# Splitting the last output panel and the next head into token halves in a two-layer transformer trunk

## Chip, cores and metric

One core of one Trainium2 chip runs the whole program. The metric is the device time of one execution in microseconds (us), median of three runs; lower is better.

## The reference, cut to what matters

The trunk has 272 tokens (16 meta tokens in front of 256), width 1024 and two layers of three sub-layers each: SwiGLU, mixer, SwiGLU. The mixer of layer 0 is stick-breaking attention, that of layer 1 sliding-window attention. Everything is float32. Each sub-layer has a norm before and a norm after:

```python
def rms_norm(x, g):
    y = x * lax.rsqrt(jnp.mean(x * x, axis=-1, keepdims=True) + RMS_EPS)
    return y * g

def swiglu(x, w_gate, w_up, w_down):
    return (jax.nn.silu(x @ w_gate) * (x @ w_up)) @ w_down

f = swiglu(rms_norm(h, g[0]), ...)
h = h + 0.5 * rms_norm(f, g[1])
m = mixer(rms_norm(h, g[2]), ...)
h = h + rms_norm(m, g[3])
f = swiglu(rms_norm(h, g[4]), ...)
h = h + 0.5 * rms_norm(f, g[5])
```

So at each of the five boundaries between sub-layers the output f of one is squared and summed over the width for each token, scaled by the inverse root, added to the residual h, and the sum is normed again for the first products of the next sub-layer. The second norm's factor depends on the token alone, so it is applied after the products.

## The kernel before, in words

Activations lie transposed: the width on the partitions, in 8 blocks of 128 (index d or k), the tokens along the free axis (272 columns; 256 where the meta tokens are no longer needed, in the output of sub-layer 4 and in sub-layer 5). Sub-layers are numbered u = 0 to 5: ffn, sb (stick-breaking), ffn, ffn, swa (sliding window), ffn.

Weights come in 156 panels of 1 MB (128 partitions by 2048). SyncE loads a panel into one of two `raw` slots (L484) as soon as the panel two before is wholly converted. ScalarE rounds it to fp32r (`w_hi`, L553, two halves of 1024 columns), and VectorE takes the rest (`w_lo`, L821, two halves). There are four converted slots, so ScalarE may start on panel g when TensorE has finished panel g - 4 (semaphore `panel_done`). Each product is made of three matmuls with fp32r operands (`three`, L1219 to L1224): w_lo with y_hi, w_hi with y_hi, w_hi with y_lo. Each of them has a weight load of its own.

An ffn sub-layer has 22 input panels (each gives 2 blocks of 128 rows, from 8 blocks k) and 11 output panels. An output panel covers 2 blocks of the hidden width and adds to all 8 output blocks d: 8 x 2 x 3 = 48 matmuls of 272 columns (`out_panel`, L1631). sb and swa have 4 output panels each with the same 48 matmuls (`out_column`, L1415; `out_unit`, L1542, 256 columns).

The boundary goes like this. During the last output panel, each block d that is done signals `f_done`. ScalarE squares the blocks (L784, L792, L797) and copies some to SBUF (L779). VectorE adds the squares (L1148 to L1164) and copies the others (L1168). After its last product TensorE sums over the partitions by multiplying with ones, in two token halves (`post_sums`, L1659 to L1665, plain float32, three calls for a half), and then runs two matmuls whose result nobody reads (L1669, `IDLE`). ScalarE turns each half's sum into the factor by Ln and Exp (L804, L807). VectorE makes y_hi of block 0 by a short way (L1176, L1180), then its y_lo (L1184, L1186), then for the other blocks the scaled output (L1197) and the new residual (L1204). ScalarE makes y_hi of it (L567) and VectorE y_lo (L833).

TensorE meanwhile waits for y_hi of block 0 and then runs the head of the next sub-layer: its first three panels at once, k by k, so that block k is needed as late as possible. For each k there are 6 tiles (3 panels x 2), with 12 matmuls on y_hi (L1287, L1289) and 6 on y_lo (L1296), all over the full 272 or 256 columns. At k = 7 a matmul with ones (L1275) sums the squares for the second norm. The fourth panel and the rest follow.

The order of each engine is written out by hand, with semaphores; instructions run in the order of the text. In an ffn sub-layer ScalarE and VectorE convert, in the loop ahead of the boundary, all three panels of the next head (`n_split`, L461); after sb and swa the third panel is converted during the boundary.

Of the kernel before, what the change touches and what calls it, by code (L numbers as in the profile page):

```python
# [25 lines left out]
P = 128  # L26
D = 1024
KT = D // P
SEQ = 256
META = 16  # L30
L = META + SEQ
# [72 lines left out]
SW_LO = [2] + [1] * 9 + [2, 2, 2]  # L104
SW_OUT = [(6, 0), (6, 1), (7, 0), (7, 1), (5, 0), (5, 1), (0, 0), (1, 0)]
SW_FILL = {6: [(0, 0), (0, 1)], 7: [(0, 2)], 8: [(1, 0), (1, 1)], 9: [(1, 2)], 10: [(0, 3), (1, 3), (2, 0)], 11: [(2, 1)]}
SW_LAST = [(2, 2), (2, 3)]
# [46 lines left out]
def bank_out(t):  # L154

    return [0, 1, 2, 3, 4, 5, 6, 7] if t.kind == "sb" else [4, 5, 6, 7, 0, 1, 2, 3]

def out_tile(ps, t, d):  # L160

    if t.kind == "swa":
        bank, half = SW_OUT[d]
        return ps[:, bank, 256 * half:256 * half + 256]
    return ps[:, bank_out(t)[d], t.t_out:L]


def out_pair(ps, t, n):

    if t.kind == "swa" and n < 3:  # L170
# [3 lines left out]
    b0 = bank_out(t)[2 * n]  # L174
    return ps[:, b0:b0 + 2, t.t_out:L]


def stays(t, d):

    return t.kind == "swa" and d < 4  # L180
# [8 lines left out]
X_ORDER = [1, 0, 2, 3, 4, 5, 6, 7]  # L189


def bank_half(t):

    return (2, 3) if t.kind == "swa" else (bank_out(t)[2], bank_out(t)[1])


def bank_idle(t):

    return 4 if t.kind == "swa" else bank_out(t)[3]
# [8 lines left out]

IDLE = 2
# [9 lines left out]
def build(nc, first_in, x_in, gains_in, sinks_in, row_in, panels_in, const_in, out):  # L219
    ctx = ExitStack()  # L220
    with ctx:
# [143 lines left out]
        f_saved2 = sem("f_saved2")  # L365
# [9 lines left out]
        part_ready = sem("part_ready")  # L375
# [85 lines left out]
        def n_split(t):  # L461

            return min(t.n_out - 1, PANELS - t.g_out - SLOTS)
# [80 lines left out]
        def _(a):  # L544
# [16 lines left out]
            def split_y(b):  # L561

                t0 = SUBS[b].t_in

                for d in range(KT if b == 0 else 1, KT):
                    a.wait_ge(x_ready, KT * (b - 1) + X_ORDER.index(d) + 1)
                    nc.scalar.activation(y_hi[:, d, t0:L], xT[:, d, t0:L], ACT.Copy,  # L567
                                         scale=gains[:, SUBS[b].pre + d:SUBS[b].pre + d + 1]).then_inc(yh_ready, 1)
                if b == 0:
                    conv_hi(2)  # L570
                    a.wait_ge(x_landed, 16)
                for c in range(2):
                    nc.scalar.activation(fT[:, 4 * c:4 * c + 4, t0:L], xT[:, 4 * c:4 * c + 4, t0:L],
                                         ACT.Square).then_inc(x_sq, 1)
# [30 lines left out]
            split_y(0)  # L605

            for t in SUBS:
# [141 lines left out]
                if t.kind == "ffn":  # L749
                    steps(a, n_split(t), lambda i, it: conv_hi(t.g_out + i + 4, it))  # L750
                elif t.kind == "sb":
                    conv_hi(t.end)
                    conv_hi(t.end + 1)
                    hi_half(t.end + 2, 0)
# [21 lines left out]
                k = t.u  # L776
                t0 = t.t_out
                def save_f(n):
                    nc.scalar.copy(fT[:, 2 * n:2 * n + 2, t0:L], out_pair(ps, t, n))\  # L779
                        .then_inc(f_saved, 3 if stays(t, 0) else 1)  # L780

                for n in range(2):
                    a.wait_ge(f_done, KT * k + 2 * n + 2)
                    nc.scalar.activation(sq[:, 2 * n:2 * n + 2, t0:L], out_pair(ps, t, n), ACT.Square)\  # L784
                        .then_inc(f_sq, 1)
                    if t.kind == "swa" and n == 0:
                        hi_half(t.end + 2, 0)
                    if not stays(t, 2 * n):
                        save_f(n)
                for d in range(4, 7):  # L790
                    a.wait_ge(f_done, KT * k + (6 if t.kind == "swa" and d == 4 else d + 1))
                    nc.scalar.activation(sq[:, d, t0:L], out_tile(ps, t, d), ACT.Square).then_inc(f_sq, 1)  # L792
                    if d == 5 and t.kind == "ffn":
                        save_f(2)
                a.wait_ge(f_done, KT * k + KT)
                for c0, c1 in token_halves(t):
                    nc.scalar.activation(sq[:, 7, c0:c1], out_tile(ps, t, 7)[:, c0 - t0:c1 - t0],  # L797
                                         ACT.Square).then_inc(f_sq, 1)
                if t.kind != "ffn":
                    save_f(2)  # L800

                for i, (c0, c1) in enumerate(token_halves(t)):
                    a.wait_ge(post_sum, 2 * k + i + 1)
                    nc.scalar.activation(post_ln[:, c0:c1], ps[:, bank_half(t)[i], c0:c1], ACT.Ln,  # L804
                                         scale=t.factor ** -2 / D).then_inc(post_log, 1)
                    a.wait_ge(post_log, 2 * k + i + 1)
                    nc.scalar.activation(post_f[:, c0:c1], post_ln[:, c0:c1], ACT.Exp, scale=-0.5).then_inc(post_ready, 1)  # L807
                if t.kind != "ffn":
                    hi_half(t.end + 2, 1)
                if t.u < 5:  # L810
                    split_y(t.u + 1)
# [3 lines left out]
        def _(v):  # L815
# [14 lines left out]
            def y_low(b, d):  # L830
                t0 = SUBS[b].t_in
                v.wait_ge(yh_ready, KT * b + d + 1)
                nc.vector.scalar_tensor_tensor(  # L833
                    out=y_lo[:, d, t0:L], in0=xT[:, d, t0:L],
                    scalar=gains[:, SUBS[b].pre + d:SUBS[b].pre + d + 1],
                    in1=y_hi[:, d, t0:L].bitcast(F32), op0=ALU.mult, op1=ALU.subtract).then_inc(yl_ready, 1)

            def pre_norm(b):
# [3 lines left out]
                v.wait_ge(x_sq, 2 * b + 2)  # L842
                for n, m in enumerate((4, 2, 1)):
                    nc.vector.tensor_tensor(fT[:, 0:m, t0:L], fT[:, 0:m, t0:L], fT[:, m:2 * m, t0:L],
                                            ALU.add).then_inc(x_acc, 1)
                    v.wait_ge(x_acc, 3 * b + n + 1)
# [32 lines left out]
            conv_lo(2)  # L879
            pre_norm(0)  # L880
# [3 lines left out]
            for t in SUBS:  # L884
# [217 lines left out]
                elif t.kind == "sb":  # L1102
                    conv_lo(t.end)
                    conv_lo(t.end + 1)
                    lo_half(t.end + 2, 0)
                if t.u == 5:
# [12 lines left out]
                    def result(n):  # L1119
# [25 lines left out]
                k, t0 = t.u, t.t_out  # L1145

                v.wait_ge(f_sq, 7 * k + 2)
                nc.vector.tensor_tensor(sq[:, 0:2, t0:L], sq[:, 0:2, t0:L], sq[:, 2:4, t0:L],  # L1148
                                        ALU.add).then_inc(f_acc, 1)
                v.wait_ge(f_acc, 4 * k + 1)  # L1150

                if t.kind == "ffn":
                    nc.vector.scalar_tensor_tensor(out=sq[:, 0, t0:L], in0=eps_ms[:, t0:L], scalar=float(KT),
                                                   in1=sq[:, 0, t0:L], op0=ALU.mult, op1=ALU.add).then_inc(f_acc, 1)
                else:
                    nc.vector.tensor_scalar(sq[:, 0, t0:L], sq[:, 0, t0:L], KT * EPS, None,
                                            ALU.add).then_inc(f_acc, 1)
                v.wait_ge(f_acc, 4 * k + 2)

                v.wait_ge(f_sq, 7 * k + 4)  # L1160
                nc.vector.tensor_tensor(sq[:, 0:2, t0:L], sq[:, 0:2, t0:L], sq[:, 4:6, t0:L],
# [625 lines left out]
```

## Time and profile before

| what | value |
|---|---|
| time, median of 3 runs | 1038.69 us (1038.0 to 1039.81) |
| profiled execution, span from first to last instruction | 1036.6 us (no other time of it is shown) |
| TensorE (PE) busy | 1024.9 us, 99% of the span, 8028 matmuls |
| weight loads (PEld) busy | 994.0 us, 96%, 8028 loads |
| VectorE (DVE) busy | 641.2 us, 62% |
| ScalarE (ACT) busy | 517.6 us, 50% |
| GpSimd (POOL) busy | 16.7 us, 2% |
| DMA | 171.26 MB, mean 165 GB/s |
| five boundaries, start of the first ones-matmul | 206.4, 342.1, 545.4, 748.7, 838.7 us |

How to read it: the profile is of one execution. Times are us from the start of its span unless ns is written. Matmuls are pipelined: the recorded length of one (0.29 us) is longer than the distance from its start to the start of the next, and it is that distance which counts when many follow each other. A matmul in plain float32 appears as two instructions, one with fp32r operands as one. The median of the runs lies 2.1 us above the profiled span.

### The profile page before, as it was taken

Reading aid. Unit: us, or ns where it says so; the run is one execution under the profiler, and the core shown is the slowest. Engines: PE = TensorE matmul, PEld = TensorE weight load, DVE = VectorE, ACT = ScalarE, POOL = GpSimd, SP = SyncE. Lnnn points to the kernel's source line nnn. Section 1 sums busy time; section 2 is a strip of 40 time slices with the busy share of each in tenths; the row PEclk is TensorE's granted clock in tenths of the full one; section 3 lists DMA queues with packets and bytes.
Section 4 is the critical chain, followed back from the end, with each engine's and each line's share of the span. In section 5 each row is a group of like instructions: output and inputs, shape, how many; then the busy total and the mean of one; then the engine's idle time right before and its main releaser. Section 6 shows DMA issues by size and latency. Waiting matters only on the chain.

```text
span 1036.6 us, 19946 instructions
## 1 busy us (share of the span) xinstructions
PE 1024.9 (99%) x8028; PEld 994.0 (96%) x8028; DVE 641.2 (62%) x893; ACT 517.6 (50%) x740; POOL 16.7 (2%) x28
## 2 busy tenths in 40 slices
PE   9999999999999999999999999999999999999997
PEld 8999999999999999999999999999998899999886
DVE  6765553478775876554447755543589777765533
ACT  5643443446675564434345544443447755544433
POOL 0000000000000000000000000000023000000000
PEclk9999999999999999999999999999999999999999
DMA  8665555514333266445542755445513335655451
GB/s 328 218 228 167 187 174 166 183 58 148 138 127 118 82 208 236 164 164 186 178 163 82 239 174 191 166 167 183 179 41 123 121 125 194 233 181 198 168 183 41
DMA packets 24533, 171.26 MB, mean 165 GB/s; under 512 B 2976, under 2 KB 2976, under 8 KB 4384
## 3 DMA queue, kind: packets, MB, share of 16 engines
q1 hardware_dynamic: 24048, 169.49, 47.4%
q8 instruction: 41, 0.67, 0.3%
q10 hardware_dynamic: 432, 1.00, 0.2%
q14 instruction: 12, 0.10, 0.0%
HBM read 169.43 MB, written 1.05 MB: 164 GB/s over the span
## 4 chain that ended last, share of the span: by engine, by line
PE 95%; DVE 2%; ACT 2%; DMA 0%; issue 0%; DVEq 0%; POOL 0%; SPq 0%; ACTq 0%; POOLq 0%
PE ps L1222 25%; PE ps L1224 25%; PE ps L1223 25%; PE ps L1287 2%; PE ps L1296 2%; PE ps L1289 2%; PE ps L1594 2%; PE ps L1595 2%; PE ps L1593 2%; PE ps L1353 1%; PE ps L1408 1%; PE ps L1527 1%; PE ps L1499 1%; PE ps L1235 1%; DMA raw<-in_panels_dram 0%; PE ps L1515 0%
## 5 line engine op out<-in xcount | busy, mean ns | idle before, releaser
L553 ACT CAST w_hi<-raw 128x1024 fp32r<-128x1024 f32 x312 | 312.7, 1047 | 393.7 <-PE ps L1224 299.4
L821 DVE TENSOR_TENSOR w_lo<-raw,w_hi 128x1024 fp32r<-128x1024 f32 x312 | 370.2, 1225 | 191.0 <-ACT w_hi L553 190.5
L1222 PE MATMUL ps<-y_hi,w_lo 128*128 128x272 f32 (+1 forms) x1454 | 420.8, 289 | 0.1
L1224 PE MATMUL ps<-y_lo,w_hi 128*128 128x272 f32 (+1 forms) x1454 | 417.8, 287 | 0.0
L1223 PE MATMUL ps<-y_hi,w_hi 128*128 128x272 f32 (+1 forms) x1454 | 416.2, 286 | 0.0
L1222 PEld LDWEIGHTS ps<-y_hi,w_lo 128*128 128x128 f32 x1454 | 273.9, 188 | 1.9 <-issue 1.1
L1223 PEld LDWEIGHTS ps<-y_hi,w_hi 128*128 128x128 f32 x1454 | 273.9, 188 | 0.3
L1224 PEld LDWEIGHTS ps<-y_lo,w_hi 128*128 128x128 f32 x1454 | 274.0, 188 | 0.0
L1222 PE MATMUL ps<-h_hi,w_lo 128*128 (+1 forms) x528 | 152.1, 288 | 0.0
L1223 PE MATMUL ps<-h_hi,w_hi 128*128 (+1 forms) x528 | 152.0, 288 | 0.0
L1224 PE MATMUL ps<-h_lo,w_hi 128*128 (+1 forms) x528 | 151.3, 286 | 0.0
L1223 PEld LDWEIGHTS ps<-h_hi,w_hi 128*128 128x128 f32 x528 | 99.4, 188 | 0.0
L1222 PEld LDWEIGHTS ps<-h_hi,w_lo 128*128 128x128 f32 x528 | 99.4, 188 | 0.0
L1224 PEld LDWEIGHTS ps<-h_lo,w_hi 128*128 128x128 f32 x528 | 99.4, 188 | 0.0
L899 DVE TENSOR_TENSOR hid<-act,ps 128x544 f32<-128x544 f32 (+1 forms) x44 | 31.2, 710 | 70.3 <-PE ps L1224 70.3
L894 DVE TENSOR_TENSOR act<-ps,rms_inv 128x544 f32<-128x544 f32 (+1 forms) x44 | 31.5, 716 | 55.7 <-PE ps L1224 50.3
L1287 PE MATMUL ps<-y_hi,w_lo 128*128 128x272 f32 (+1 forms) x210 | 54.3, 291 | 3.4 <-DVE y_hi L1180 2.8
L1289 PE MATMUL ps<-y_hi,w_hi 128*128 128x272 f32 (+1 forms) x210 | 53.2, 286 | 0.0
L1287 PEld LDWEIGHTS ps<-y_hi,w_lo 128*128 128x128 f32 x210 | 39.5, 188 | 6.5 <-DVE y_hi L1180 4.9
L1289 PEld LDWEIGHTS ps<-y_hi,w_hi 128*128 128x128 f32 x210 | 39.5, 188 | 0.0
L567 ACT ACTIVATE y_hi<-xT,gains 128x272 fp32r<-128x272 f32 (+1 forms) x35 | 18.2, 521 | 35.1 <-DVE xT L1204 35.1
L1594 PE MATMUL ps<-w_hi,h_hi 128*128 128x512 f32 x88 | 34.7, 395 | 0.0
(192 smaller groups left out, 1051.4 us busy)
## 6 DMA issues: line engine op xcount, KB each, us to landing
raw<-in_panels_dram SPq DMA_DIRECT2D x156, 1024.0 KB, 4.9
first<-in_first_dram SPq DMA_DIRECT2D x3, 784.0 KB, 6.8
xT<-in_x_dram SPq DMA_DIRECT2D x1, 1088.0 KB, 13.4
out_dram<-fT SPq DMA_DIRECT2D x4, 256.0 KB, 2.0
const<-in_const_dram ACTq DMA_DIRECT2D x1, 920.0 KB, 10.2
first<-in_first_dram SPq DMA_DIRECT2D x2, 392.0 KB, 3.6
gain_row<-in_row_dram SPq DMA_DIRECT2D x1, 512.0 KB, 5.5
gains<-in_gains_dram ACTq DMA_DIRECT2D x1, 48.0 KB, 3.6
```

The lines of the kernel that those rows point to most:

```text
L553: nc.scalar.copy(w_hi[:, g % SLOTS, part], raw_part(g, part)).then_inc(hi_ready, 1)
L821: nc.vector.tensor_tensor(w_lo[:, g % SLOTS, part], raw_part(g, part), w_hi[:, g % SLOTS, part].bitcast(F32), ALU.subtract).then_inc(lo_re ...
L894: nc.vector.tensor_tensor(act[:, j % 2, :, t0:L], ps[:, b0:b0 + 2, t0:L], spread(rms_inv, 2, t0), ALU.mult).then_inc(gate_ready, 1)
L899: nc.vector.tensor_tensor(hid[:, j % 2, :, t0:L], act[:, j % 2, :, t0:L], ps[:, b0:b0 + 2, t0:L], ALU.mult).then_inc(h_ready, 1)
L1222: nc.tensor.matmul(dst, w_lo[:, slot, pc], yh, start=first, stop=False, skip_group_check=shared)
L1223: nc.tensor.matmul(dst, w_hi[:, slot, pc], yh, start=False, stop=False, skip_group_check=shared)
L1224: return nc.tensor.matmul(dst, w_hi[:, slot, pc], yl, start=False, stop=last, skip_group_check=shared)
L1287: nc.tensor.matmul(dst, w_lo[:, g % SLOTS, pc], y_hi[:, k, c0:L], start=(k == 0), stop=False)
L1289: nc.tensor.matmul(dst, w_hi[:, g % SLOTS, pc], y_hi[:, k, c0:L], start=False, stop=False)
L1296: nc.tensor.matmul(ps[:, BANK_IN[i][c], c0:L], w_hi[:, g % SLOTS, pc], y_lo[:, k, c0:L], start=False, stop=False)
L1593: nc.tensor.matmul(dst, hh[:, cols], w_lo[:, slot, at:at + 512], start=first, stop=False)
L1594: nc.tensor.matmul(dst, hh[:, cols], w_hi[:, slot, at:at + 512], start=False, stop=False)
```

## The change

The last output panel runs over the left token half for all 8 blocks d and then over the right half (136 columns each, 128 in swa), instead of once over all columns. The three ones-calls of the left half come after the third or fourth block of the right half, those of the right half after the first k of the next head's left half. The head's first two k (`SPLIT = 2`) run in halves too: left on y_hi, left on y_lo, right on y_hi, right on y_lo; k = 2 to 7 stay whole. At the boundary after swa one of the six tiles, (2, 0), runs its first two k whole and late. ScalarE and VectorE square, add, save and scale in halves where the halves are apart. The second half of the third head panel is converted later, after the fourth step over the blocks, and after an ffn sub-layer its first half too comes at the start of the boundary. The squares for the second norm are made in four pairs instead of two fours. The idle matmuls are gone. Banks in PSUM are dealt out anew: blocks 6 and 7 (4 to 7 in swa) are read by VectorE from PSUM instead of from a copy. The core of the diff:

```diff
-            return min(t.n_out - 1, PANELS - t.g_out - SLOTS)
+            return min(t.n_out - 2, PANELS - t.g_out - SLOTS)
...
+                def last_panel():
+
+                    k, g = t.u, t.end - 1
+                    pe.wait_ge(lo_ready, 2 * g + 2)
+                    for half, (c0, c1) in enumerate(token_halves(t)):
+                        for d in range(KT):
+                            if half == 1:
+                                if stays(t, d) or t.kind == "swa" and d >= 4:
+                                    pe.wait_ge(f_sq, 10 * k + (3 if d < 6 else 5 if t.kind == "swa" else d - 2))
+                                elif d // 2 == 1:
+                                    pe.wait_ge(f_saved_d, 2 * k + 1)
+                                else:
+                                    pe.wait_ge(f_saved, 4 * k + (1 if d < 2 else 2))
+                                if t.kind != "swa" and d == KT - 1:
+                                    pe.wait_ge(post_log, 2 * k + 1)
+                            for c in range(2):
...
+                                mm = three(out_tile(ps, t, d)[:, c0 - t0:c1 - t0], g % SLOTS, D * c + P * d, hh, hl,
+                                           False, c == 1, shared=True)
                             mm.then_inc(f_done, 1)
...
-                    if t.u < 5:
-                        for _ in range(IDLE):
-                            nc.tensor.matmul(ps[:, bank_idle(t), t0:L], cst("ones"), sq[:, 0, t0:L], start=True, stop=True)
+                            if half == 1 and d == SUM_AFTER[t.kind]:
+                                post_sums(t, 0)
...
+                    for k in range(SPLIT):
+                        pe.wait_ge(yha_ready, Y_LEFT * n + k + 1)
+                        for tile in early:
...
+                            mm = head_part(tile, k, left, 0, first=(k == 0))
+                            if k == 0 and tile == (0, 0):
+                                mm.then_inc(panel_done, 1)
+                            head_part(tile, k, left, 1)
+                        if k == 0:
+                            post_sums(prev, 1)
+                    for k in range(SPLIT):
+                        pe.wait_ge(yla_ready, SPLIT * n + k + 1)
+                        for tile in early:
+                            head_part(tile, k, left, 2)
+                    for k in range(SPLIT):
+                        pe.wait_ge(yh_ready, KT * t.u + k + 1)
+                        for tile in early:
+                            head_part(tile, k, right, 0)
+                            head_part(tile, k, right, 1)
+                    for k in range(SPLIT):
                         pe.wait_ge(yl_ready, KT * t.u + k + 1)
...
+                        for tile in early:
+                            head_part(tile, k, right, 2)
+                    for tile in late:
+                        pe.wait_ge(post_log, 2 * n + 2)
+                        for k in range(SPLIT):
+                            for part in range(3):
+                                head_part(tile, k, (t0, L), part, first=(k == part == 0))
+                    for k in range(SPLIT, KT):
...
```

ScalarE's new order at the boundary:

```diff
+                hi_half(t.end + 2, 0)
+                square_pair(0, 0)
+                square_pair(1, 0)
+                save_pair(0, 0)
+                square_pair(2, 0)
...
+                    square_tile(6, 0)
+                    square_tile(7, 0)
+                    save_pair(2, 0)
+                square_pair(0, 1)
+                square_pair(1, 1)
+                factor(0)
+                save_pair(1, 1)
+                square_pair(2, 1)
...
+                    save_pair(2, 1)
+                    square_tile(6, 1)
+                    square_tile(7, 1)
+                y_high(k + 1, 0)
+                factor(1)
+                y_high(k + 1, 1)
```

and VectorE's:

```diff
+                lo_half(t.end + 2, 0)
+                add_squares(0)
+                add_last(0)
+                save_pair(1, 0)
+                fold(0)
+                save_pair(0, 1)
+                add_squares(1)
...
+                first_high(0)
                 u_of(0)
...
+                x_of(0)
+                add_last(1)
+                fold(1)
+                first_low(0)
+                y_low(b, 1, 0)
+                v.wait_ge(f_saved_d, 2 * k + 1)
+                u_of(1)
+                x_of(1)
+                first_high(1)
+                u_of(2)
+                x_of(2)
+                first_low(1)
```

## Rows read from the trace of the kernel before

**Rows 1.** The page, part 1 and the granted clock over 40 slices.

```profile
PE 1024.9 (99%) x8028; PEld 994.0 (96%) x8028; DVE 641.2 (62%) x893; ACT 517.6 (50%) x740; POOL 16.7 (2%) x28
...
PEclk9999999999999999999999999999999999999999
```

**Rows 2.** The page, chain that ended last, shares by engine.

```profile
PE 95%; DVE 2%; ACT 2%; DMA 0%; issue 0%; DVEq 0%; POOL 0%; SPq 0%; ACTq 0%; POOLq 0%
```

**Rows 3.** Waits of TensorE: total us, times, longest.

```profile
PE ps L1287 <- DVE y_hi L1180: 2.8, 5, 0.6
```

**Rows 4.** Timeline, first boundary: start, length, engine, line.

```profile
202.82 0.29 PE L1224 MATMUL ps<-h_lo,w_hi 128*128 128x272 f32 x1
...
206.18 0.28 PE L1224 MATMUL ps<-h_lo,w_hi 128*128 128x272 f32 x1
...
207.22 0.31 PEld L1659 LDWEIGHTS ps<-sq,const 128*128 128x128 f32 x2
...
207.91 0.76 PEld L1669 LDWEIGHTS ps<-sq,const 128*128 128x128 f32 x4
...
209.66 0.39 PE L1287 MATMUL ps<-y_hi,w_lo 128*128 128x272 f32 x1 [0.55 <-DVE y_hi L1180]
...
210.01 0.28 PE L1287 MATMUL ps<-y_hi,w_lo 128*128 128x272 f32 x1
...
211.26 0.92 PE L1296 MATMUL ps<-y_lo,w_hi 128*128 128x272 f32 x6
...
212.63 0.29 PE L1287 MATMUL ps<-y_hi,w_lo 128*128 128x272 f32 x1
```

**Rows 5.** Timeline, fifth boundary (after swa).

```profile
838.54 0.28 PE L1224 MATMUL ps<-sw_lo,w_hi 128*128 128x256 f32 x1
...
842.80 0.28 PE L1287 MATMUL ps<-y_hi,w_lo 128*128 128x256 f32 x1
...
843.98 0.87 PE L1296 MATMUL ps<-y_lo,w_hi 128*128 128x256 f32 x6
...
845.32 0.28 PE L1287 MATMUL ps<-y_hi,w_lo 128*128 128x256 f32 x1
```

**Rows 6.** Timeline, running sums of sb: fp32r matmuls of 64 columns among wider ones.

```profile
241.85 0.19 PE L1393 MATMUL ps<-sp_hi,sums_w 128*128 128x64 f32 x1
241.85 0.19 PEld L1395 LDWEIGHTS ps<-sp_hi,sums_w 128*128 128x128 f32 x1
241.88 0.27 PE L1395 MATMUL ps<-sp_hi,sums_w 128*128 128x64 f32 x1
241.96 0.19 PEld L1385 LDWEIGHTS ps<-sp_lo,sums_w 128*128 128x128 f32 x1
241.99 0.36 PE L1385 MATMUL ps<-sp_lo,sums_w 128*128 128x256 f32 x1
242.07 0.19 PEld L1387 LDWEIGHTS ps<-sp_lo,sums_w 128*128 128x128 f32 x1
242.19 0.28 PE L1387 MATMUL ps<-sp_lo,sums_w 128*128 128x256 f32 x1
```

**Rows 7.** Groups of ACT and DVE by line: busy us, mean ns, idle before.

```profile
L553 ACT CAST w_hi<-raw 128x1024 fp32r<-128x1024 f32 x312 | 312.7, 1047 | 393.7 <-PE ps L1224 299.4
L821 DVE TENSOR_TENSOR w_lo<-raw,w_hi 128x1024 fp32r<-128x1024 f32 x312 | 370.2, 1225 | 191.0 <-ACT w_hi L553 190.5
...
L792 ACT ACTIVATE sq<-ps 128x272 f32<-128x272 f32 (+1 forms) x15 | 5.9, 405 | 1.3 <-PE ps L1224 1.1
...
L807 ACT ACTIVATE post_f<-post_ln 128x136 f32<-128x136 f32 (+1 forms) x10 | 3.1, 315 | 0.3
...
L1180 DVE TENSOR_TENSOR y_hi<-sq,pre_ms 128x136 fp32r<-128x136 f32 (+1 forms) x10 | 3.0, 298 | 0.3
L1176 DVE SCALAR_TENSOR_TENSOR sq<-fT,gg,post_f 128x136 f32<-128x136 f32 x8 | 2.8, 356 | 3.5 <-ACT post_f L807 3.5
```

**Rows 8.** DMA issues: size and median us from issue to landing.

```profile
raw<-in_panels_dram SPq DMA_DIRECT2D x156, 1024.0 KB, 4.9
```

More of the change, by code:

```diff
@@ L173, in out_pair @@
         return ps[:, 0:2, 0:256]
-    b0 = bank_out(t)[2 * n]
-    return ps[:, b0:b0 + 2, t.t_out:L]
+    return ps[:, 2 * n:2 * n + 2, t.t_out:L]
 def stays(t, d):
-    return t.kind == "swa" and d < 4
+    return d >= (4 if t.kind == "swa" else 6)
 def token_halves(t):
@@ L775, in _ @@
                     break
[L776 to L798, printed above, removed]
@@ new lines, in _ @@
+                if t.kind == "swa":
+                    square_pair(3, 1)
+                else:
+                    save_pair(2, 1)
[4 more added lines that the diff above has]
+                y_high(k + 1, 1)
+                for i in range(2, X_OPS):
+                    if X_ORDER[i][0] > 0:
+                        y_high(k + 1, i)
+                    if i == 3:
+                        hi_half(t.end + 2, 1)
+                    for n, after in SQUARES:
+                        if after == X_ORDER[i][0] and i >= 4:
+                            if n == 0:
+                                a.wait_ge(x_ready, X_OPS * k + 8)
+                            x_square(n, t0)
@@ L814, in _ @@
+                norm_x(k + 1)
         @block.vector
@@ new lines, in _ @@
+                v.wait_ge(f_saved, 4 * k + (2 if t.kind == "swa" else 4))
+                u_of(3)
+                x_of(3)
+                y_low(b, 1, 1)
+                u_of(4)
+                y_low(b, 2)
+                x_of(4)
+                u_of(5)
+                x_of(5)
+                y_low(b, 3)
+                lo_half(t.end + 2, 1)
+                for i in range(6, X_OPS):
+                    u_of(i)
+                    x_of(i)
+                    if i != 8:
+                        y_low(b, {6: 4, 7: 5, 9: 6}[i])
+                    else:
+                        add_pair(b, 0)
@@ new lines, in head_part @@
+                def head_part(tile, k, cols, part, first=False, last=False):
+                    i, c = tile
+                    g, (c0, c1) = t.g0 + i, (max(cols[0], first_col(t, i)), cols[1])
+                    if part == 0:
+                        pe.wait_ge(lo_ready, 2 * g + 1 + k // 4)
+                    pc = slice(256 * k + P * c, 256 * k + P * c + P)
+                    return nc.tensor.matmul(ps[:, BANK_IN[i][c], c0:c1], (w_lo if part == 0 else w_hi)[:, g % SLOTS, pc],
+                                            (y_lo if part == 2 else y_hi)[:, k, c0:c1], start=first, stop=last,
+                                            skip_group_check=True)
```

409 lines of the change are left out of this document (222 added, 187 removed).

## The prediction

> **What bounds the kernel now.** I read the page first. TensorE is busy for 99% of the span at the full granted clock (9 in all 40 slices, 2.4 GHz) [rows 1], and the chain that ended last lies on it for 95% [rows 2]. So a microsecond of TensorE work costs a microsecond, and only its pauses can be won. The list of its waits gives 2.8 us in five waits for y_hi of block 0, one for each boundary [rows 3]. That list understates them, since the ones-matmuls and the idle ones fill most of the pause. So I took the pause from the timeline [rows 4]: 202.82 to 206.18 holds 27 products, which gives 0.1244 us from start to start. The last product of sub-layer 0 starts at 206.18 and the third of the next head at 210.01. Less three distances that is 3.46 us without products. A second, small pause stands before k = 1: the six y_lo matmuls start at 211.26, so the ninth start after that should be at 212.26 (eight distances) and is at 212.63, 0.38 us late. The next three boundaries show 3.46 to 3.47 and 0.35 to 0.43. The one after swa has 256 columns and a distance of 0.118 us (ten in 842.80 to 843.98); its pause is 842.80 - 838.54 - 3 x 0.118 = 3.91 us, and 845.32 - 843.98 - 8 x 0.118 = 0.40 follow [rows 5]. Together 4 x 3.46 + 3.91 + 4 x 0.38 + 0.40 = 19.7 us.
>
> **What is removed.** The ones-calls stay: three for a half take 207.22 to 207.91 = 0.69 us [rows 4], six 1.38, and at five boundaries 6.9 us. If products cover all the rest, 19.7 - 6.9 = 12.8 us go. That is the whole prize. The idle matmuls are inside it: four instructions issued from 207.91, over before y_hi arrives at 209.66, so they cost nothing, and taking them out gives nothing of its own. The clock was full on both sides of the pause, and in the new order no pause of that length is left in which it could fall.
>
> **What is added: matmuls.** The last panel is 48 matmuls at full width, and becomes 96 at half width. The head's first two k are 2 x 6 x 3 = 36 and become 72 (at the fifth boundary one tile stays whole: 30 become 60). Over five boundaries 5 x 48 + 4 x 36 + 30 = 414 whole ones go and 828 halves come. The columns are the same; the number of weight loads doubles, since each matmul has its own load (8028 and 8028) [rows 1]. Of the whole ones 324 have 272 columns (four panels of 48, three heads of 36, 24 of the head of swa) and 90 have 256 (the other 12 of that head, 78 at the fifth boundary): 324 x 0.1244 + 90 x 0.118 = 50.9 us.
>
> What does a half cost? The trace has no 136-column fp32r matmul. The nearest rows are two of 64 columns in the running sums [rows 6]. The first starts at 241.85, and the next is let in at 241.88: 64 columns stream in 0.03 us, so narrow fp32r is not slower for each column. But its weights are being loaded from 241.85, the next load begins at 241.96 and the one after at 242.07: 0.11 us from load to load, though the matmuls between them need 0.03. The loads set the pace. Seen in four such places the two steps take 0.22 or 0.23, so **0.1125 us for each half**, against 0.1244 for a whole. A half streams in 136/64 x 0.027 = 0.057 us, well under the load, and cannot go below it. Bounds: 0.107 (the shortest step that the two-digit rows allow) to 0.118 (the distance at 256 columns [rows 5]). The far end below is the half's own streaming plus what a whole one has over its columns: 272 columns at the rate of rows 6 are 0.113, so 0.011 on top, 0.068 in all. The far end above is a ones-call of 136 columns, 0.69 / 3 = 0.23 us [rows 4]. I take 0.1125, because rows 6 are the same type, the same 128x128 weights and the only place where a matmul is shorter than its load.
>
> 828 x 0.1125 = 93.2 us, less 50.9: **+42.3 us**, of which 24.5 in the panels and 17.8 in the heads. Net 42.3 - 12.8 = **+29.5 us**.
>
> The Trainium skill speaks to this in "TensorE: Matmul & The Clock Gate". Its section "LDWEIGHTS (loading the stationary operand)" has a load take its columns divided by 1.2 GHz, 107 ns for 128; rows 6 agree (0.11 us). Its section "Back-to-back issue gap" is milder: about 81 ns for each load and matmul pair at 128 columns. By that figure the sum would be 828 x 0.081 - 50.9 - 12.8 = +3.4 us instead of +29.5; rows 6 speak against it, and no other row bears on it.
>
> **Do the other engines keep up?** Count from the start of the last panel, at 0.1125. The left half ends at 5.4 us, three blocks of the right take 2.0, the sums 0.7, the other five 3.4: the head's first product is due at 11.5. ScalarE converts half a panel first (1.05 [rows 7]), then squares pairs as they come (0.41 for 272 elements). With the left's last square at 5.9, a copy, the right's first pair to 7.4 and its second, released by block 3 of the right half at 8.8, to 9.4, Ln (about 0.3) and Exp (0.32) end at 10.0. VectorE needs 0.36 + 0.30 [rows 7] and a passing of semaphores, so y_hi of block 0, left, is there at about 11.0, 0.5 before it is due. The right sums need the last square (12.0) at 12.8 and the added squares (12.4) at 13.3. y_hi of block 1, left, comes at 12.3 and is due at 13.5; the right half of block 0 at 15.2, due at 16.2; that of block 1 at 16.2, due at 17.6. From k = 2 a step is 18 x 0.1244 = 2.24 us for TensorE and some 1.4 for VectorE, as before. The moved conversion costs ScalarE 1.05 and VectorE 1.23 us once [rows 7] near k = 3, and its result is first needed at k = 4, 3 us later. The load that this releases, panel end + 4, takes 4.9 us [rows 8] and its slot is read more than 10 us later. SyncE and GpSimd issue nothing else. So the terms are priced at nothing under that cover, with margins of 0.5 to 1 us; if the ScalarE line slips (the queue behind the wait for the left sums holds the right half's squares), each boundary waits 0.5 to 1.5 us more. The four pairs of squares instead of two fours add two instructions off the path.
>
> **The sum.** Profiled span 1036.6 + 29.5 = 1066.1 us. The median of the runs is 2.1 above that span, so 1038.7 + 29.5 = **1068.2 us**. With 0.107 and 0.118 for a half it is 1063.6 and 1072.8.
>
> **Rivals.**
> 1. Weights are loaded ahead and a half costs its own streaming, 0.068 us. Then 828 x 0.068 = 56.3, +5.4 - 12.8 = -7.4: **1031 us**, faster. It decides below (50.9 + 12.8) / 828 = 0.077 us for a half. For it: the recorded length of a load, 0.19 us, is longer than the distance, so loads do overlap matmuls. Against it: rows 6, where two short matmuls in a row did not bring the loads closer than 0.11. And at that pace the pair of ScalarE and VectorE would be late at block 0 and give part of it back, up to no change. Chance 0.06 faster, 0.03 within 0.2%.
> 2. Loads overlap in part, and a half costs between 0.077 and 0.107 us: at the middle, 0.092, it is 76.2 - 50.9 - 12.8 = +12.5, **1051 us**. For it: rows 6 are only two matmuls long, and a long row of short ones may settle at a closer pace. Chance 0.06. The 81 ns of the Trainium skill's section "Back-to-back issue gap" would lie at its lower end.
> 3. The forecast's load pace, and the margins of the paragraph above are not there: a wait of 0.5 to 1.5 us at each boundary on y_hi of block 0 or on the right half's sums, **1071 to 1076 us**. For it: five engine hand-overs in the chain. Chance 0.15.
> 4. Narrow fp32r is as slow as the ones-calls: 828 x 0.23 - 50.9 - 12.8 = +127, **1165 us**. Rows 6 speak against it (64 columns in 0.03 us). Chance 0.04.
>
> **How the numbers follow.** The forecast has 0.66. Two runs of this kernel can be told apart above 0.2% (2.1 us). Faster by more: 0.06. Within: 0.03. Slower: 0.66 + 0.15 + 0.06 + 0.04 = 0.91. The range takes in the forecast's bounds, nearly all of rival 3, and some room below for a load pace slightly under 0.107: 1055 to 1078 holds about 0.8.
>
> **What would show it.** In the changed kernel's profile: PE and PEld instructions both up by 414 less the 20 idle ones; 96 matmuls of 136 columns over about 10.8 us in each last panel (6.0 before), 0.11 apart; loads of 128x128 back to back without gaps there; no wait for y_hi of block 0 at a boundary; from the start of the last panel to the end of k = 7 some 34 us (28 before). If the half-width matmuls stand less than 0.077 apart, the forecast is wrong in sign; if TensorE shows idle stretches at the boundary, the margins are wrong; if the whole-width matmuls change their distance, the cause lies elsewhere.

## The result, and the profile after

The changed kernel takes **1068.76 us** (median of 4 runs, 1067.69 to 1069.14) against 1038.76 for the kernel before in the same session (4 runs). The ratio is 1.0287, with an interval of 1.0273 to 1.0302: slower, by 30.0 us, where 29.5 were forecast. The profiled execution has a span of 1067.3 us and took 1069.12.

The page of the changed kernel, its span, the busy times and the granted clock [rows 1], and the shares of the chain that ended last [rows 2]:

```profile
span 1067.3 us, 20900 instructions
...
PE 1056.7 (99%) x8422; PEld 1030.6 (97%) x8422; DVE 650.9 (61%) x954; ACT 522.2 (49%) x780; POOL 16.8 (2%) x28
...
PEclk9999999999999999999999999999999999999999
...
PE 97%; ACT 1%; DVE 1%; DMA 1%; issue 0%; DVEq 0%; SPq 0%; ACTq 0%
```

PE and PEld both went up by 394, which is the forecast 414 less the 20 idle ones. TensorE was the bound before and is it still, at the full clock. A share of 99% before and after says nothing of whether the work in it got dearer; the distances do. TensorE's waits in the changed kernel [rows 3]:

```profile
PE ps L1356 <- ACT y_hi L605: 1.5, 1, 1.5
PE ps L1340 <- POOL post_ln L503: 1.1, 1, 1.1
PE ps L1327 <- DVE qkv L961: 0.9, 1, 0.9
PE ps L1543 <- DVE sp_lo L994: 0.6, 1, 0.6
PE ps L1657 <- DVE qkv L1086: 0.6, 1, 0.6
```

The five waits for y_hi at the boundaries are gone. L1356 lies in the first sub-layer, which the change does not touch. L961 (first tile of sb behind its head) and L1086 (the scores of swa) are new; where they come from stands in the part on why the prediction was right. The timeline of TensorE over the first boundary [rows 4]:

```profile
201.02 0.23 PE L1327 MATMUL ps<-h_hi,w_lo 128*128 128x136 f32 x1
...
201.19 0.28 PE L1329 MATMUL ps<-h_lo,w_hi 128*128 128x136 f32 x1
...
206.22 0.28 PE L1329 MATMUL ps<-h_lo,w_hi 128*128 128x136 f32 x1
...
208.34 0.44 PE L1455 MATMUL ps<-sq,const 128*128 128x136 f32 x2
...
212.27 0.27 PE L1329 MATMUL ps<-h_lo,w_hi 128*128 128x136 f32 x1
212.38 0.28 PE L1383 MATMUL ps<-y_hi,w_lo 128*128 128x136 f32 x1
...
233.23 0.62 PE L1444 MATMUL ps<-fT,const 128*128 128x272 f32 x2
...
235.04 0.29 PE L1383 MATMUL ps<-y_lo,w_hi 128*128 128x272 f32 x1
236.22 0.36 PE L1327 MATMUL ps<-y_hi,w_lo 128*128 128x272 f32 x1 [0.89 <-DVE qkv L961]
```

From 201.19 to 206.22 there are 45 steps, so a half takes **0.1118 us**; a whole one took 0.1244. The panel's last product stands at 212.27 and the head's first at 212.38, one ordinary distance apart: the pause is gone. Yet the stretch from the panel's first half to the last product of k = 7 takes 34.02 us (201.02 to 235.04), where the same work took 28.20 before (200.33 to 228.53). The same rows of the kernel before, with its ones-matmul for the second norm (L1275):

```profile
200.33 0.29 PE L1222 MATMUL ps<-h_hi,w_lo 128*128 128x272 f32 x1
...
225.97 0.62 PE L1275 MATMUL ps<-fT,const 128*128 128x272 f32 x2
...
228.53 0.28 PE L1224 MATMUL ps<-y_lo,w_hi 128*128 128x272 f32 x1
228.95 0.36 PE L1222 MATMUL ps<-y_hi,w_lo 128*128 128x272 f32 x1
```

The left factor and y_hi on their engines, on the timeline of ACT and DVE:

```profile
210.51 0.32 ACT L810 ACTIVATE post_f<-post_ln 128x136 f32<-128x136 f32 x1
...
211.54 0.30 DVE L1241 TENSOR_TENSOR y_hi<-sq,pre_ms 128x136 fp32r<-128x136 f32 x1
...
233.89 0.44 DVE L895 TENSOR_SCALAR pre_ms<-ps 128x272 f32<-128x272 f32 x1 [2.04 <-PE ps L1444]
...
235.34 1.99 DVE L961 TENSOR_TENSOR qkv<-ps,rms_inv 128x544 f32<-128x544 f32 x3 [0.68 <-PE ps L1383]
```

y_hi of block 0 ends at 211.84 and is due at 212.38. The overlap does what it was made for, with 0.54 us to spare.

### The profile page after: what moved, and what is told of

It is laid out like the page before. It is cut to its first block, busy times and chain, and to the rows that moved or that the text cites. A ratio compares the mean times of both kernels' runs of the same rounds, so it can differ in the third digit from the quotient of the medians.

```text
span 1067.3 us, 20900 instructions
## 1 busy us (share of the span) xinstructions
PE 1056.7 (99%) x8422; PEld 1030.6 (97%) x8422; DVE 650.9 (61%) x954; ACT 522.2 (49%) x780; POOL 16.8 (2%) x28
## 4 chain that ended last, share of the span: by engine, by line
PE 97%; ACT 1%; DVE 1%; DMA 1%; issue 0%; DVEq 0%; SPq 0%; ACTq 0%
PE ps L1327 25%; PE ps L1329 25%; PE ps L1328 25%; PE ps L1383 10%; PE ps L1748 2%; PE ps L1749 2%; PE ps L1747 2%; PE ps L1511 1%; PE ps L1566 1%; PE ps L1685 1%; DMA first<-in_first_dram 1%; PE ps L1657 1%; PE ps L1673 0%; PE ps L1356 0%; PE ps L1364 0%
## 5 line engine op out<-in xcount | busy, mean ns | idle before, releaser
L1327 PE MATMUL ps<-y_hi,w_lo 128*128 128x272 f32 (+1 forms) x1424 | 411.7, 289 | 0.9 <-DVE qkv L961 0.9
L1328 PE MATMUL ps<-y_hi,w_hi 128*128 128x272 f32 (+1 forms) x1424 | 408.0, 287 | 0.0
L1328 PEld LDWEIGHTS ps<-y_hi,w_hi 128*128 128x128 f32 x1424 | 268.6, 189 | 0.1
L1329 PEld LDWEIGHTS ps<-y_lo,w_hi 128*128 128x128 f32 x1424 | 268.5, 189 | 0.0
L1327 PE MATMUL ps<-h_hi,w_lo 128*128 (+2 forms) x576 | 164.9, 286 | 0.0
L1328 PE MATMUL ps<-h_hi,w_hi 128*128 (+2 forms) x576 | 164.8, 286 | 0.0
L1329 PE MATMUL ps<-h_lo,w_hi 128*128 (+2 forms) x576 | 164.1, 285 | 0.0
L1383 PE MATMUL ps<-y_hi,w_lo 128*128 128x272 f32 (+4 forms) x298 | 75.3, 287 | 0.0
L1383 PE MATMUL ps<-y_hi,w_hi 128*128 128x272 f32 (+4 forms) x298 | 73.8, 282 | 0.0
L1383 PEld LDWEIGHTS ps<-y_hi,w_hi 128*128 128x128 f32 x298 | 56.7, 190 | 0.2
L1383 PE MATMUL ps<-y_lo,w_hi 128*128 128x272 f32 (+4 forms) x298 | 46.3, 282 | 0.0
L1383 PEld LDWEIGHTS ps<-y_lo,w_hi 128*128 128x128 f32 x298 | 40.0, 190 | 0.0
```

The costliest lines, as they stand in the source:

```text
L1327: nc.tensor.matmul(dst, w_lo[:, slot, pc], yh, start=first, stop=False, skip_group_check=True)
L1328: nc.tensor.matmul(dst, w_hi[:, slot, pc], yh, start=False, stop=False, skip_group_check=True)
L1329: return nc.tensor.matmul(dst, w_hi[:, slot, pc], yl, start=False, stop=last, skip_group_check=True)
L1383: return nc.tensor.matmul(ps[:, BANK_IN[i][c], c0:c1], (w_lo if part == 0 else w_hi)[:, g % SLOTS, pc], (y_lo if part == 2 else y_hi)[:, k ...
```

## The experiments

The eleven kernels below go after two questions: what do the halves cost, and what does each removed or kept pause cost? The prediction's theory is that each matmul, however narrow, costs the 0.11 us of its weight load, and that the pauses are worth 12.8 us. Lengths of a pause are given below from the start of the last product to the start of the head's first, if nothing else is said: 3.48 us for the kernel before (206.18 to 209.66 [rows 4]).

**The idle matmuls, alone.** Kernel before, with

```diff
-                    if t.u < 5:
+                    if False:
                         for _ in range(IDLE):
```

> The kernel before without its two idle matmuls at each boundary, nothing else changed. My theory (they lie wholly in the wait for y_hi of block 0 and the clock does not need them): same as before, 1038.8 us within 1 us; product-free pause still 3.46 us, granted clock 1.0. Rival (they keep the clock up, or they delay the head): a lower granted clock after the pause and a longer time by 1 us or more for each boundary, 5 us in all; or a shorter pause, up to 1 us less each, 1034 us.

Measured: 1038.28 us against 1038.58, ratio 0.9996 [0.9987, 1.0004]; mean granted clock 0.999. Taking them out moves nothing that the runs can tell, and the clock holds over a pause of the old length (3.48 us at the first boundary). That edit is worth nothing, as priced.

**The halves, alone.** Kernel before, each matmul of the last panel cut in two token halves side by side; no order is changed, nothing overlaps.

```diff
+def cut_three(dst, slot, col, yh, yl, first, last, shared=False):
+    n = dst.shape[-1] // 2
+    for c in (slice(0, n), slice(n, 2 * n)):
+        mm = three(dst[:, c], slot, col, yh[:, c], yl[:, c], first, last, shared=True)
+    return mm
...
-                            mm = three(ps[:, bank_out(t)[d], t0:L], g % SLOTS, D * c + P * d,
+                            mm = (cut_three if last else three)(
+                                       ps[:, bank_out(t)[d], t0:L], g % SLOTS, D * c + P * d,
...
```

> The kernel before, with only the last output panel's 48 matmuls cut into a left and a right half, each block's two halves right behind each other, so that nothing can overlap that did not before. This prices the halves by themselves: 240 whole ones (29.6 us) become 480 halves. Theory (each half waits for its weight load, 0.1118 us as in the changed kernel): 480 x 0.1118 = 53.7, +24.1 us, 1062.9 us. Rival (a half costs by its columns, 0.068 us): 32.6 us, +3.1, 1042 us. Pause at the boundary unchanged at 3.46 us in both.

Measured: 1060.64 us, ratio 1.0208 [1.0189, 1.0226], +22.1. Its timeline, first boundary:

```profile
205.31 0.27 PE L1224 MATMUL ps<-h_lo,w_hi 128*128 128x136 f32 x1
...
210.67 0.27 PE L1224 MATMUL ps<-h_lo,w_hi 128*128 128x136 f32 x1
...
213.98 0.39 PE L1293 MATMUL ps<-y_hi,w_lo 128*128 128x272 f32 x1 [0.55 <-DVE y_hi L1180]
```

48 steps in 5.36 us: 0.1117 again, in the old order, without any of the rest. That shows the cause of most of the loss by itself. At this pace the five panels cost 480 x 0.1117 = 53.6 us instead of 29.5, +24.1. Some came back: the slower panel lets ScalarE and VectorE catch up. The pause is 3.30 to 3.31 us where it was 3.47 to 3.48 at four boundaries, and 3.24 where it was 3.92 after swa, 1.4 us less in all. This execution also reached its first panel 0.35 us sooner (18.53 us against 18.88). 24.1 - 1.4 - 0.35 = 22.4, which is the difference of the spans (1059.0 - 1036.6).

**Narrower still.** Changed kernel, the right half of the last panel run over half its columns (68, or 64 in swa). It leaves out the products of the last quarter of the tokens with the last panel.

```diff
                     for half, (c0, c1) in enumerate(token_halves(t)):
+                        if half == 1:
+                            c1 = (c0 + c1) // 2
                         for d in range(KT):
```

> The changed kernel, with the right half of the last output panel cut from 136 to 68 columns (64 of 128 in swa): the products of the last quarter of the tokens with the last panel are left out. The count of matmuls and loads is the same. Theory (the load sets the pace): no change from the changed kernel, 1068.8 us within 1.5 us, distance still 0.112 us. Rival (columns set a part of the pace): 240 matmuls x 68 columns x 0.42 ns = 6.8 us less, 1062 us.

Measured: 1096.28 us, ratio 1.0565 [1.052, 1.0611], mean clock 0.972. The time is a miss by 27.5 us. The timeline, then the windows (the columns: PE, PEld, DVE, ACT and POOL busy, granted clock, DMA share, GB/s), of this kernel:

```profile
210.10 0.28 PE L1327 MATMUL ps<-h_hi,w_lo 128*128 128x68 f32 x1
...
211.11 0.28 PE L1327 MATMUL ps<-h_hi,w_lo 128*128 128x68 f32 x1
...
211.87 0.41 PE L1383 MATMUL ps<-y_hi,w_hi 128*128 128x136 f32 x1
212.08 0.41 PE L1383 MATMUL ps<-y_hi,w_lo 128*128 128x136 f32 x1
```

```profile
206.00:212.00 6.00, 6.00 (x53) 6.00 (x52) 2.87 (x9) 2.86 (x10) 0.00 (x0) 0.94 0.00 0
212.00:218.00 6.00, 6.00 (x30) 6.00 (x29) 2.83 (x11) 1.33 (x6) 0.00 (x0) 0.50 0.00 0
218.00:224.00 6.00, 6.00 (x30) 6.00 (x30) 5.86 (x15) 3.31 (x7) 0.00 (x0) 0.50 0.00 0
```

68 columns stand 0.112 us apart (nine steps in 1.01), as far as 136. So the width below 136 does not enter. No run has a matmul without a load of its own; that it is the load that costs, and not a fixed price of each matmul, rests on rows 6, where two matmuls of 64 columns start 0.03 us apart and the loads behind them 0.11. But near the end of this row of 48 matmuls, which began at 205.43, the granted clock goes from 2.4 to 1.2 GHz and the distance from 0.11 to 0.21 us, although PE and PEld are busy for every microsecond of the windows. It happens at the first, second and fifth boundary, and the clock stays down for some 20, 17 and 24 us, 61.4 us together. At 0.213 us for a half instead of 0.112 each of these microseconds loses 0.47 of its work: 29 us by this estimate, against 28.1 between the spans (1095.4 and 1067.3). So the clock is all of this miss.

**The second pause of before.** Kernel before; VectorE scales block 1 (`u_of(1)`) only after the new residual of block 0, so that ScalarE gets y_hi of block 1 earlier. A second kernel takes the idle matmuls out as well.

```diff
-                    u_of(i + 1)
+                    if i > 0:
+                        u_of(i + 1)
...
+                    if i == 0:
+                        u_of(1)
```

> The kernel before, with one step of VectorE moved: the scaled output of the second block (u_of(1)) comes after the new residual of the first (x_of(0)) instead of before it. The second small pause of each boundary, about 0.38 us before k = 1, waits for ScalarE's y_hi of block 1, which waits for that residual. Theory: the residual comes about 0.4 us earlier, the small pause goes, nothing else is late: 5 x 0.38 = 1.9 us less, 1036.9 us, under both kernels. Rival (the queue behind it is late instead: the next residual and y_hi of block 2): the same pause turns up before k = 2, no change, 1038.8 us.

> The kernel before with both small edits, the moved step of VectorE and no idle matmuls. Theory: the two do not touch each other, and the time is that of the moved step alone, about 1037.7 us, 0.1% under the kernel before. Rival (with the idle ones gone, the clock falls behind some boundary in some runs): runs of 1045 us and more among them.

Measured: 1037.65 us, ratio 0.9993 [0.9983, 1.0004], and 1037.54, ratio 0.9997 [0.9988, 1.0006]. In the first one's timeline k = 1 goes on from its first product at 211.66 and its third at 212.02; with no pause the third would be due at 210.88 + 8 x 0.1245 = 211.88. So 0.14 us are left of 0.38. From the last product of sub-layer 0 to that of sub-layer 1 it is 135.66 us against 135.83, so 0.17 of it are kept. But 5 x 0.24 = 1.2 us is at the edge of what the runs can tell, and both intervals include no change.

**Head: one block in halves.** Changed kernel, `SPLIT = 1`.

```diff
-SPLIT = 2
+SPLIT = 1
-Y_LEFT = SPLIT + 1
+Y_LEFT = 3
-                        pe.wait_ge(yla_ready, SPLIT * n + k + 1)
+                        pe.wait_ge(yla_ready, 2 * n + k + 1)
```

> The changed kernel with only k = 0 of the next head in halves; k = 1 runs whole (y_hi and y_lo of block 1 are still made in halves). 87 whole matmuls come back for 174 halves: 174 x 0.1118 - 87 x 0.124 = 8.7 us less work. Theory (halves cover the post-norm at about the price of the cover): TensorE now waits about 1 us at each boundary for the right half of y_hi of block 0, so 5 of the 8.7 are given back: 1065 us. Rival (the cover of k = 0 alone is enough): no wait, 1060 us. Rival (the overlap matters more than the halves cost): slower than 1068.8.

Measured: 1065.47 us, ratio 1.0258 [1.0236, 1.0279]; clock 0.999. A wait appears on y_hi of block 0's right half:

```profile
PE ps L1383 <- DVE y_hi L1241: 4.6, 5, 1.0
```

Half of the head's 174 cuts are undone. By the measured 0.1118 each was worth some 0.1 us (0.2236 - 0.1244), 8.7 us in all, and 4.6 of them come back as waits; that leaves 4.1, and the medians differ by 3.3. Undoing the halves wins even where it uncovers a wait.

**Head: no halves.** Changed kernel, `SPLIT = 0`; the right ones-calls stand ahead of the head, and the waits that the first k carried are put there.

```diff
-SPLIT = 2
+SPLIT = 0
...
+                    post_sums(prev, 1).then_inc(panel_done, 1)
+                    pe.wait_ge(f_saved_d, 2 * n + 2)
...
+                    pe.wait_ge(post_log, 2 * n + 2)
                     for tile in late:
```

> The changed kernel with the whole head at full width; only the last output panel is in halves, and the left half's sums and factor are made beside the right half's products. 174 whole matmuls come back for 348 halves: 17.4 us less work. Theory: the pause for the right half's sums, factor and y_hi comes back, about 2.6 us at each boundary, 13 us, so the net is -4 to -5: 1064 us; granted clock stays at 1.0. Rival (the early left half shortens the pause to under 1 us each): 1056 us or less.

Measured: 1066.03 us, ratio 1.0262 [1.0225, 1.0299]; clock 0.995; the wait for y_hi is 8.7 us in five. That is 2 us above what was expected, and the clock, expected at 1.0, is enough to make it: the two runs at 0.998 took 1064.31 and 1064.9 us, those at 0.995 and 0.992 took 1067.17 and 1070.35. In the profiled one it fell at the first three boundaries, for some 3.4 us each. At the first boundary the last product stands at 211.28, the pause is 3.15 us, and the head starts at half the clock (0.43 us long and 0.22 apart, where 272 columns otherwise stand 0.124 apart):

```profile
214.43 0.52 PE L1383 MATMUL ps<-y_hi,w_lo 128*128 128x272 f32 x1 [1.73 <-DVE y_hi L1241]
214.75 0.43 PE L1383 MATMUL ps<-y_hi,w_hi 128*128 128x272 f32 x1
214.97 0.43 PE L1383 MATMUL ps<-y_hi,w_lo 128*128 128x272 f32 x1
```

**Last panel whole.** Changed kernel, the last panel over all columns (the head still in halves); ScalarE waits once more before it squares over banks that VectorE reads.

```diff
-                    for half, (c0, c1) in enumerate(token_halves(t)):
...
+                    for d in range(KT):
+                        for c in range(2):
...
+                            mm = three(out_tile(ps, t, d), g % SLOTS, D * c + P * d, hh, hl, False, c == 1, shared=True)
+                        mm.then_inc(f_done, 9 if d == KT - 1 else 1)
+                    post_sums(t, 0)
```

> The changed kernel with the last output panel at full width; the first two k of the head stay in halves. 240 whole matmuls come back for 480 halves: 24.1 us less work. Both halves' squares now start together behind the whole panel. Theory: a pause of about 2.6 us before the head's left half, 13 us in all, so the net is -10 to -11: 1058 us. Rival (the squares and sums of both halves queue up on ScalarE, and the pause is as long as the half panel was, 5 us each): no gain, 1068 us.

Measured: 1086.87 us, ratio 1.0468 [1.0428, 1.0509]; clock 0.976. This is 29 us above what was expected, and 18 above the kernel it was made from. Page (granted clock in 40 slices), timeline behind the second boundary and windows there:

```profile
PEclk9999999999999699999996999999999969999999
```

```profile
349.39 0.33 PE L1384 MATMUL ps<-y_hi,w_lo 128*128 128x136 f32 x1 [1.56 <-DVE y_hi L1242]
...
350.68 0.27 PE L1384 MATMUL ps<-y_hi,w_hi 128*128 128x136 f32 x1
...
352.15 0.41 PE L1384 MATMUL ps<-y_hi,w_lo 128*128 128x136 f32 x1
352.37 0.41 PE L1384 MATMUL ps<-y_hi,w_hi 128*128 128x136 f32 x1
```

```profile
347.00:351.00 4.00, 2.44 (x20) 2.24 (x21) 3.24 (x11) 2.90 (x11) 0.00 (x0) 1.00 0.00 0
351.00:357.00 6.00, 6.00 (x31) 6.00 (x31) 5.08 (x17) 2.92 (x7) 0.00 (x0) 0.52 0.01 1
```

The last product ahead of the pause stands at 346.21, so the pause is 3.18 us. The matmuls behind it are at first 0.11 apart, and from 351.67 on more than 0.2: the clock falls behind the pause, after the first 12 halves, and stays down for some 17 us. The same happens at the third and fifth boundary. At the first and the fourth, with pauses of 3.18 and 3.17 us, it held. So the expected sum stood on a term that had been priced at nothing. Whether the clock is really the whole of it, the next run asks.

**Last panel whole, with idle matmuls.** The same, and in the pause

```diff
+                    pe.wait_ge(f_saved_d, 2 * k + 2)
+                    for _ in range(4):
+                        nc.tensor.matmul(ps[:, 0, t0:L], cst("ones"), cst("cos", P, t0, L), start=True, stop=True,
...
```

> panel_whole with four matmuls of ones with the cosine table put back into TensorE's wait (272 columns, plain float32, 0.45 us each, result not read), behind the left half's sums. In panel_whole the granted clock fell to 0.5 for 12 to 20 us behind three of the five boundaries. Theory (pause and half-width matmuls together left TensorE too little work, and the clock, not the pause, made up the 29 us above my 1058): the clock stays at 1.0 and the time comes down to 1058 to 1062 us. Rival (the idle matmuls do not hold the clock, since the half-width head behind them is what lets it fall): still 1080 us or more with a mean clock under 0.98.

Measured: 1057.91 us, ratio 1.0187 [1.0172, 1.0203]; clock 0.999. The windows of the same stretch:

```profile
347.00:351.00 4.00, 3.68 (x22) 3.17 (x23) 2.92 (x10) 3.25 (x12) 0.00 (x0) 1.00 0.00 0
351.00:357.00 6.00, 6.00 (x56) 6.00 (x55) 5.01 (x17) 2.64 (x6) 0.00 (x0) 1.00 0.00 1
```

56 matmuls in 6 us instead of 31, and 29.0 us less in all, for 20 matmuls whose result nobody reads. The clock was the whole of the miss: 1057.91 is what the sum without it gave. The idle matmuls are not quite free here, since they run on past the arrival of y_hi: the pause is 3.44 to 3.45 us at the first four boundaries, where it was 3.17 to 3.18, 1.1 us in all. It also gives the panel's own account, free of the clock: against the changed kernel the spans differ by 1067.3 - 1056.3 = 11.0 us. The halves' price of 480 x 0.1118 - 29.5 = 24.2 us goes. The pause comes back, on this kernel's timeline 206.07 to 209.52, less one distance 3.33 us; 0.69 of it are ones-calls that the changed kernel has too, so 5 x 2.64 = 13.2. The difference is 11.0. That the two agree to the tenth is luck: the changed kernel's profiled execution reached its first panel 0.8 us later (19.57 against 18.77), and without that the spans differ by 10.2.

**Neither in halves.** Changed kernel with both edits: what remains is the new order of ScalarE's and VectorE's work. Once as it is, once with idle matmuls in both waits (four and three).

```diff
+                    post_sums(prev, 1).then_inc(panel_done, 1)
+                    for _ in range(3):
+                        nc.tensor.matmul(ps[:, 0, prev.t_out:L], cst("ones"), cst("cos", P, prev.t_out, L), start=True, stop=True,
...
```

> The changed kernel with neither the panel nor the head in halves on TensorE; ScalarE and VectorE keep the new order, with squares, copies and factors in halves, and the third head panel converted late. It removes all 828 halves and keeps everything else of the change. Theory (the halves on TensorE are what costs, 41.6 us; the rest costs only through a longer pause, about 5.7 us at each boundary against 3.8 before, since the new queues are written for overlap): 1050 us, up to 1056. Rival (something else in the change costs, such as the late conversion or the new bank order): above 1060 us.

> both_whole with matmuls of the same kind in its two waits, four behind the left half's sums and three behind the right half's. Its mean granted clock of 0.984 means some 34 us at half clock, which cost up to 17 us. Theory: clock 1.0, 1047 to 1050 us, with only the longer pause of the new queues left against 1038.8. Rival (the clock fell for another cause, such as the whole-width head on narrower work before it): no change, 1064 us.

Measured: 1063.82 us, ratio 1.0236 [1.0217, 1.0255], clock 0.984; with the idle matmuls 1052.99, ratio 1.0141 [1.0126, 1.0157], clock 1.0. Again the clock was the miss, 10.8 us of it. The clock was down for some 7 us at each of the five boundaries. The second kernel is still 3 us above the upper end of what was expected and 14.7 above the kernel before in its session (1038.30). Its timeline, first boundary:

```profile
205.66 0.28 PE L1330 MATMUL ps<-h_lo,w_hi 128*128 128x272 f32 x1
...
207.37 2.10 PE L1826 MATMUL ps<-const 128*128 128x272 f32 x8
...
210.47 1.54 PE L1426 MATMUL ps<-const 128*128 128x272 f32 x6
212.37 0.36 PE L1384 MATMUL ps<-y_hi,w_lo 128*128 128x272 f32 x1 [0.36 <-DVE y_hi L1242]
```

From the last product to the first of the head are 6.71 us, against 3.48 before [rows 4]. All five boundaries together have 33.5 us against 17.8, 15.7 more. The idle matmuls do not make it so: without them the first boundary has 6.70 us too. The second pause (1.9) is gone, and the two waits of L961 and L1086 (1.4, below) stay: 15.2, where the spans differ by 14.6. So the new order, with its two passes over the factor, costs some 15 us by itself, and pays only under products that cover it.

## Why the prediction was right, by its steps

- **The half.** Forecast 0.1125 us from two matmuls of 64 columns [rows 6]; measured 0.1118 in the changed kernel (45 steps), 0.1117 in the old order (48 steps), 0.112 at 68 columns. The halves cost 828 x 0.1118 = 92.6 us, net of the whole ones +41.7, where +42.3 were forecast. Rivals 1, 2 and 4 fall with it (0.068, below 0.107, 0.23). By the Trainium skill, "TensorE: Matmul & The Clock Gate", section "LDWEIGHTS (loading the stationary operand)", a load takes its columns divided by 1.2 GHz, which gives an estimate of 107 ns for 128 columns; the measured 0.1118 lies 5 ns above it. The about 81 ns for a load and a matmul of 128 columns in the Trainium skill's section "Back-to-back issue gap" do not hold for these fp32r matmuls. The trace has 0.1118 us over 45 steps of 136 columns, and the same over 69 steps of exactly 128 in the last panel of swa (7.70 us). By an estimate from the 81 ns this change would have come out near +3 us instead of +30.
- **The prize.** 12.8 us, wholly collected: no wait for y_hi, and 212.27 to 212.38 is one distance. At the first boundary the three terms give 168 x 0.1118 - 84 x 0.1244 = +8.33 for the halves and 3.84 - 1.38 = 2.46 off for the pauses, +5.87; measured 34.02 - 28.20 = +5.82.
- **Do the other engines keep up.** y_hi of block 0 was forecast 11.0 us after the panel's start and due at 11.5. It came at 10.8 and was due at 11.4. Rival 3 (waits of 0.5 to 1.5 at each boundary) did not happen.
- **The idle matmuls at nothing.** Shown for the kernel before, and right for the changed kernel (clock 1.0). The sentence that no pause is left in which the clock could fall was right in its result and argued too easily: the kernel with 68 columns, which has no pause either, lost some 28 us to the clock. The step should have said what a fall would cost.
- **What was missed.** Two waits were not priced. The first tile of sb stands 1.18 us behind the last product of the head (235.04 to 236.22) where it was 0.42, +0.76; at the scores of swa it is 0.88 (802.74 to 803.62) where it was 0.22, +0.66. The trace shows where both come from, though no run tried it. The ones-matmul that sums the squares for the second norm at k = 7 stood ahead of all six tiles before (L1275 at 225.97, 18 products behind it) and stands behind the second tile now (L1444 at 233.23, 12 products behind it). VectorE starts on its sum 0.65 us after it in both (226.62 and 233.89), and on qkv, which TensorE waits for, 1.46 and 1.45 us later. So the second norm's factor comes six products later than before, measured from the end of the head, and 6 x 0.1244 = 0.75 is the 0.76. At the head of swa it is the same: from that ones-matmul to the head's last product there were 2.54 us (767.99 to 770.53) and are 1.79 now (793.52 to 795.31). The profiled execution also reaches its first panel 0.7 us later (L1356's wait; the runs' spans go from 1065.9 to 1067.3). 41.7 - 12.8 + 1.4 + 0.7 = 31.0 against a difference of spans of 30.7, and 30.0 in the medians. So the mechanism was right, and part of the closeness of 29.5 to 30.0 is luck: 0.6 us too much for the halves stood against 1.4 us of waits that had no term, and the 0.7 us belong to that one execution.

## What to carry to other kernels

Before you cut a product to cover a pause, price the cut: here a half costs 0.1118 us and a whole one 0.1244, since each matmul loads its own weights, so a cut matmul that covers 0.1118 us of a pause costs 0.0992 more and can at best win 0.0126. A busy share of 99% hides this; the distance from start to start shows it. And before you move or uncover a pause on TensorE, look at the granted clock of the changed kernel and not only at the lengths: two of the variants lost 29 and some 28 us to it, more than twice the 12.8 us that the edit set out to win, and a third lost 11.

## What was unexpected of the hardware

- The granted clock fell to its lower level (1.2 of 2.4 GHz) with TensorE busy without a break: at the end of a row of 48 products of 68 columns, 0.112 us apart, at three of five boundaries; windows at 0.50, and some 28 us in all. With 136 columns at the same distance it held (the changed kernel, 1.0).
- A pause of 3.48 us between rows of whole products did not bring it down, even without idle matmuls (0.999). One of 3.17 to 3.27 us between whole products and halves did at three of five boundaries (0.976) and held at two. Between halves and whole products, in the kernel whose head stays whole, the clock fell at pauses of 3.15, 3.10 and 3.15 us and held at 3.15 and 3.58 in the same execution. Pauses of 6.7 to 7.0 us, with six ones-calls in them, brought it down at all five. Idle matmuls in these waits kept it at 0.999 and 1.0. So the length of the pause alone does not decide; what does is open.
- How long it stayed down differed: some 3.4 us in the kernel with a whole head (the window 214.50:217.80 at 0.50, 218.00:222.00 at 1.00), some 17 us in the one with a whole panel, where the first two k of the head in halves run behind the fall (351.30:368.20 at 0.50, 368.40:372.00 at 1.00). No run varies this by itself.
- It is not the same from one execution to the next: the kernel with the whole panel took 1080.97 us at a mean clock of 0.976 and 1090.14 at 0.967, the one with 68 columns 1092.15 at 0.976 and 1105.39 at 0.964. With the idle matmuls the whole-panel kernel stayed within 1057.58 to 1058.15.
